# One projection piece of the last head, computed in step 5 instead of step 4

## What is computed

```python
h = x * (1 + sc1) + sh1
proj = h @ w_in
q, k, v, u, gates = jnp.split(proj, ...)          # 8 heads, gates for pooling and attention
q, k = rope(q), rope(k)
o = attend(q, k, v, lam)                          # softmax(q1 k1) - lam * softmax(q2 k2), causal, blocks of 128 queries
attn_out = head_rmsnorm(o, subln_g) * (1.0 - lam_init)
g_pool, g_attn = jnp.split(jax.nn.sigmoid(gates), 2)
merged = g_pool * pool_out + g_attn * attn_out
x = layer_norm(alpha * x + (1 + g1) * (merged @ w_out), ln1_g, ln1_b)
x = layer_norm(alpha * x + (1 + g2) * hier_moe(h2, ...), ln2_g, ln2_b)
```

## Time and profile before

| | us |
|---|---|
| median of 3 runs | 1370.22 |
| lowest and highest | 1365.11, 1373.54 |
| the profiled execution | 1374.49 |
| its span in the trace | 1372.7 |
| TensorE busy | 1260.1 (92%) |
| VectorE busy | 993.4 (72%) |
| ScalarE busy | 731.7 (53%) |
| GpSimd busy | 123.2 (9%) |

### The profile page before, as it was taken

How to read it: one execution, slowest core, us unless ns; L and a number is a source line. 1 busy time by engine, 2 the same in 40 slices (tenths; PEclk the granted TensorE clock), 3 DMA queues, 4 the chain that set the end, 5 groups by cost and what they waited for, 6 DMA issues and landing times.

```text
span 1372.7 us, 25410 instructions
## 1 busy us (share of the span) xinstructions
PE 1260.1 (92%) x9182; PEld 1097.2 (80%) x9182; DVE 993.4 (72%) x1497; ACT 731.7 (53%) x1309; POOL 123.2 (9%) x83
## 2 busy tenths in 40 slices
PE   5898999999999999999999987999399999999966
PEld 4788989998999989999899874877278887888832
DVE  3644456677575775757757666799879998999948
ACT  2344334454544445345454454323359898899835
POOL 0433100000000000000000000000021111111042
PEclk9799999999999999999999998999579999999978
DMA  9988345354373543735437345363377999565776
GB/s 326 293 275 257 110 119 113 89 82 125 92 140 88 86 125 89 139 88 82 131 85 142 110 116 162 95 218 150 124 260 271 342 327 359 183 214 181 275 250 201
DMA packets 221389, 237.35 MB, mean 173 GB/s; under 512 B 26530, under 2 KB 193282, under 8 KB 221155
## 3 DMA queue, kind: packets, MB, share of 16 engines
q1 hardware_dynamic: 206035, 181.28, 46.7%
q0 software_dynamic: 6976, 25.23, 5.6%
q10 hardware_dynamic: 8280, 29.51, 5.4%
HBM read 180.90 MB, written 46.85 MB: 166 GB/s over the span
## 4 chain that ended last, share of the span: by engine, by line
PE 65%; DVE 15%; DMA 6%; ACT 5%; SPq 4%; issue 3%; POOL 0%; ACTq 0%; DVEq 0%; POOLq 0%
PE AB L1088 9%; PE AB L1089 9%; PE AB L1092 9%; PE S L977 6%; PE S L979 6%; PE S L978 6%; PE S L1191 3%; ACT F L1596 3%; DMA F<-rms_d 2%; PE T L1217 2%; ACT R L1596 2%; PE OB L977 1%; DVE sm L2176 1%; PE OB L978 1%; PE OB L979 1%
## 5 line engine op out<-in xcount | busy, mean ns | idle before, releaser
L1088 PE MATMUL AB<-R 128*128 128x344 f32 x960 | 315.2, 332 | 1.2 <-ACT F L1596 1.2
L1089 PE MATMUL AB<-R 128*128 128x344 f32 x960 | 305.5, 322 | 0.0
L1596 ACT ACTIVATE R<-F 128x1024 fp32r<-128x1024 f32 (+3 forms) x290 | 282.3, 1023 | 31.7 <-ACT F L1596 15.7
L977 PE MATMUL S<-R 128*128 128x512 f32 x480 | 192.6, 401 | 3.2 <-ACT F L1596 1.6
L979 PE MATMUL S<-R 128*128 128x512 f32 x480 | 188.2, 392 | 0.0
L978 PE MATMUL S<-R 128*128 128x512 f32 x480 | 188.1, 392 | 0.0
L1088 PEld LDWEIGHTS AB<-R 128*128 128x128 f32 x960 | 182.4, 190 | 5.6 <-issue 3.0
L1089 PEld LDWEIGHTS AB<-R 128*128 128x128 f32 x960 | 182.8, 190 | 0.0
L1596 ACT ACTIVATE F<-AB 128x344 f32<-128x344 f32 (+3 forms) x129 | 59.0, 460 | 230.8 <-PE AB L1092 208.1
L1092 PE MATMUL AB<-R 128*128 128x344 f32 x960 | 172.0, 321 | 0.0
L1092 PEld LDWEIGHTS AB<-R 128*128 128x128 f32 x960 | 156.2, 188 | 0.0
(11 more groups left out here) (309 smaller groups left out, 2145.3 us busy)
## 6 DMA issues: line engine op xcount, KB each, us to landing
F<-in_w_ada SPq DMA_DIRECT2D x24, 1024.0 KB
F<-in_w_in SPq DMA_DIRECT2D x44, 512.0 KB
F<-in_w_e_gate SPq DMA_DIRECT2D x16, 1024.0 KB
F<-in_w_e_up SPq DMA_DIRECT2D x16, 1024.0 KB
F<-in_w_e_down SPq DMA_DIRECT2D x16, 1024.0 KB
y_d<-F ACTq DMA_DIRECT2D x32, 512.0 KB
out<-F SPq DMA_DIRECT2D x24, 512.0 KB, 4.0
F<-F SPq DMA_DIRECT2D x192, 43.0 KB, 1.9
```

The source lines that it names most:

```text
L977: mm(out, w[0], m[1], start=start, stop=False)
L1088: mm(bank[:, 0:PIECE], whl[b][0][:, k, :], x[1][:, k, :], start=(k == 0), stop=False)
L1089: mm(bank[:, 0:PIECE], whl[b][0][:, k, :], x[0][:, k, :], start=False, stop=False)
L1596: return nc.scalar.activation(out, in_, func, **kw)
```

## The change

The sixth piece of the last head goes from the list of step 4 to that of step 5.

```diff
         if h == H - 1:
-            return [first + j for j in ((0,), (1,), (2,), (3,), (4, 5), (), (), ())[i]]
+            return [first + j for j in ((0,), (1,), (2,), (3,), (4,), (5,), (), ())[i]]
```

## The result

| | us |
|---|---|
| before, median of 9 runs | 1369.13 (1365.06 to 1373.54) |
| changed, median of 9 runs | 1375.26 (1372.60 to 1379.24) |
| ratio | 1.0048, 95% interval 1.0033 to 1.0062 |
| profiled execution, span before and changed | 1372.7 and 1374.0 |

The ratio is 6.6 us of 1369.13, with an interval of 4.5 to 8.5 us. The two spans differ by less, because the first traced execution of before was one of its longest (1374.49 us): in it L2375 of head 7, which on VectorE stands ahead of everything that the change can delay, comes at 816.15, in the changed kernel's at 813.27. Times inside the stretch are therefore compared from L2375 on.

The account below looks back on a forecast made before the run. VectorE was taken to set the pace in this stretch, with TensorE early. A 5.7 us gate delay plus 1.7 us of clock gave +7.4 us on 1370.22, so 1377.6 us, range 1371 to 1385.

Parts of the forecast that it names:

- VectorE sets the pace, TensorE is early: Last head, 810.98 to 819.14: chain entries are all VectorE work, while TensorE waits 4.19 us ahead of scores(6).
- Step 1: TensorE in step 4 idles 1.2 us ahead of product(7,2), then 2.9 us ahead of the page rows; price 0.
- Steps 2 and 3: Piece ends in step 5 at 820.97; w_out_hi(0) waits for it, so w_out_lo(0) starts 5.74 us later on the chain.
- The forecast sign that ScalarE would idle some 6 us: ScalarE's copy to `wo` would have an idle of some 6 us ahead of it, released by TensorE's L1092.
- Step 4: ScalarE's 0.46 us copy of the piece, after page_exps in step 5, fits into a vanished wait; price 0.
- Step 5: The moved piece on TensorE falls partly to half clock behind two waits: 1.7 us, bounds 0 and 3.87.
- A: Rival: delay stays, but the slow TensorE stretch 838.60 to 845.00 does not recur; +2.7 us, 1372.9; 10%.
- B: Rival: the piece fills TensorE's 4.19 us wait and step 4 shortens; at most -3.9 us, 1366.3; 4%.
- C: Rival: a second slow TensorE stretch falls on step 6, 3.0 us more; +10.4 us, 1380.6; 8%.

Follow-up runs that it names:

- e1: Changed kernel with w_out_hi(0) and w_out_lo(0) moved to step 5, behind its exponentials and maxima, the piece staying in step 5; ratio to before 1.0015.
- e4: Kernel before with only w_out_lo(0) moved on VectorE, behind the maxima and page_max of step 5; ratio to before 1.0006.
- e3: Changed kernel with the sixth piece ahead of the page rows in step 5; ratio to before 1.0037.
- e5: Kernel before with the sixth piece still in step 4 but behind product(7,2); ratio to before 1.0007.
- e9: Changed kernel with the sixth piece computed twice, 24 matmuls more; ratio to before 1.0064.
- e10: Kernel before with the sixth piece computed twice in step 4, 24 matmuls more; ratio to before 1.0017.
- e8: Second run of the changed kernel with only w_out_lo(0) moved on VectorE, behind the maxima and page_max of step 5; ratio to before 1.0021.
- e2: Changed kernel with only w_out_lo(0) moved on VectorE, behind the maxima and page_max of step 5, first run; ratio to before 1.0052.
- e7: Changed kernel with all eight w_out_lo on GpSimd in place of VectorE; ratio to before 1.0069.
- e6: Kernel before with all eight w_out_lo on GpSimd in place of VectorE; ratio to before 1.0033.
- e12: Changed kernel, unaltered, traced a second time; from L2375 to the exponentials of step 5 it took 10.38 us.

## Why the prediction was right, step by step

*VectorE sets the pace, TensorE is early.* Right: without the gate the exponentials come as soon as VectorE allows, whatever TensorE idles in front of its product and page rows (e1, e4).

*Step 1, the lost cover costs nothing.* Right: idles of 1.2 and 2.9 us were forecast, 1.17 and 2.88 came, and e1 keeps both with **a** at 1.88 us.

*Steps 2 and 3, the gate.* Right: `w_out_lo(0)` was to come 5.74 us later, VectorE idled 5.74 us, and by **a** the delay of the exponentials is 5.84. That the first trace agrees to the hundredth is luck, since its piece stayed at full clock; in the second the two are 7.28 and 7.36. e3, e5, e9 and e10 move **b** with the opening of the gate. The forecast sign that ScalarE would idle some 6 us ahead of `w_out_hi(0)` was wrong; it idled 10.51, since the copy that used to stand in between had left.

*Step 4, the copy is free.* Right: it stands at 824.34, ahead of `merged_hi(0)`, which now waits for nothing, and the low parts of step 5 run at 827.20 for 2.34 us as before, without a gap.

*Step 5, the clock, 1.7 us.* This is the term that was mis-sized, in what it adds to the time, and its place was only half right. The half clock in the piece is real but not fixed: it came in the second trace of the changed kernel (1.54 us in **b**), in e8 and e1, not in the first trace, e2, e7 or e9. Where it came, the parts behind took less: against the first trace steps 6 and 7 gave back 0.85 and 0.58 us, and **c** came out equal. Where it stayed away, half clock in step 6 added 0.90 us, a place at which the prediction's sum had nothing. And step 7 moved by 1.37 us between the two traces of before. The stretch **c** grew by 5.6 to 7.0 us, depending on which trace of before is taken, so all that the clock adds to the gate's 5.8 lies between -0.3 and +1.2 us, below the 1.7.

*The sum.* Forecast were +7.4 us, 1377.6 us. The medians differ by 6.1, the ratio says 6.6 with 4.5 to 8.5. The measured 1375.26 is 2.3 below, 1.1 of it because the median of before came down to 1369.13 with more runs. 5.7 alone and 7.4 both lie in the interval, so the times do not say how much of the clock term is in them. The prediction held that a measurement tells only changes of about 1% from none; with nine runs of each kernel the interval is narrower and leaves out zero.

*The rivals.* A, the delay given back: **c** is at least 5.6 us longer, not 2.7. Its premise did occur in part, but in the kernel before: in the second trace the way from step 7's maxima to L2557 was 1.37 us shorter, with less half clock, and no change was needed for it. B, a gain of 3.9 us, falls with e1. C, a second slow stretch in step 6, came in the first trace with 0.90 us, not 3.0; its +10.4 lies above the interval of the ratio.

What stays open is why e2, e3 and e4 took 1 to 4 us more by their medians than **c** of their traces. e8 puts a good part of it down to scatter; two traces or one of each kernel do not settle the rest. That scatter lies outside the stretch too: behind L2557, where these kernels are alike, the traces still took from 496.7 to 500.8 us.

## What to carry to other kernels

When work is moved into an engine's wait, look first at who waits for its end, and where that waiter stands in its own queue. A gate that was 0.4 us from its condition can be the head of two queues, and then the moved work lands on the path at full length. The wait of an engine that is early (here 4.19 us of TensorE) was not room that could be sold: what counted was the engine which it waits for. And a lead of one or two microseconds is better priced in a stretch of the trace between two fixed instructions than in medians that scatter by as much; but take two traces, since the stretch itself moved by up to 1.5 us with TensorE's clock.

## What the runs showed of the hardware

GpSimd and VectorE exclude each other for some operations. While GpSimd subtracts two SBUF tensors (2.34 us, e6), VectorE's L2374, L2386 and L2387 rose from 0.17, 0.15 and 0.34 us to 1.67, 2.13 and 2.40; step 7's L2347 and L2348, with no GpSimd operation beside them, kept their 0.75 and 1.28. Not every operation is held up: the L2353 at 852.29, from a PSUM and an SBUF tile, lies inside a GpSimd operation (850.73, 2.40 us) and took its 0.69 us. The Trainium skill, SBUF — State Buffer, section Who interferes with whom, says that the two engines share one pair of ports as a lock, held for the whole instruction, against VectorE operations with two SBUF inputs or in a two-port mode; this trace agrees, L2353 included. Which mode the VectorE operations with one SBUF tensor (L2387, L2347) ran in, the trace does not say.

Where TensorE's half clock falls differs between executions of one kernel. The same instructions, behind the same idles of 1.17, 2.88 and 6.04 us, were granted 0.69 in the piece and then 1.00 in step 7 in one execution, and 1.00 and then 0.74 in the other (e12 and the first trace). In this pair and in that of e2 and e8 a slow piece was followed by parts that took less, so the stretch as a whole moved by 0.10 and 0.40 us only. It is no rule: the first trace of before is later than its second at L2375 (816.15 and 814.55) and also took 1.35 us more behind it.
